# Final residual of a two-layer trunk step: state rows stored to the outputs early, expert rows added there by accumulating transfers

## The reference

```
def trunk_layer(x, cond, p, mixer, rope, ctx):
    sh1, sc1, g1, sh2, sc2, g2 = adaln(cond, p['w_ada'], p['b_ada'])
    h = rms_norm(x, p['g_norm1']) * (1 + sc1) + sh1
    y, state = mixer(h, p, rope, ctx)
    x = x + g1 * y
    h = rms_norm(x, p['g_norm2']) * (1 + sc2) + sh2
    x = x + g2 * hier_moe(h, p)
    return x, state
```

## Time and profile before

| | us |
|---|---|
| median of three runs | 1000.05 |
| the runs | 1000.92, 995.45, 1000.05 |
| the profiled execution | 995.68 |
| its span | 993.9 |

### The profile page before, as it was taken

One profiled execution on the slowest core, in us unless ns is written; L12 is line 12 of the kernel. 1 busy time (PEld: TensorE's weight loads), 2 busy tenths in 40 slices (PEclk: granted clock), 3 DMA queues, 4 the chain that ended last, 5 costly groups with the idle time before them and its releaser, 6 DMA issues.

```text
span 993.9 us, 14410 instructions
## 1 busy us (share of the span) xinstructions
PE 894.8 (90%) x5457; PEld 499.1 (50%) x5457; DVE 407.2 (41%) x1184; ACT 239.6 (24%) x604; POOL 120.1 (12%) x131
## 2 busy tenths in 40 slices
PE   4999889999999999887899998998989999997880
PEld 2345436547555565444356564555655555544440
DVE  2102476346622442211363666564764225321214
ACT  3111144111111111111344455333211111111111
POOL 1000000100222222211100000001001222222120
PEclk9999999999999999999999999999999999998995
DMA  9989799739899999998760029606699999999965
GB/s 374 399 333 404 289 421 416 257 137 363 350 417 417 410 417 418 418 418 315 278 233 6 1 94 377 260 1 189 217 420 400 417 419 408 417 416 419 413 276 197
DMA packets 61685, 318.85 MB, mean 321 GB/s; under 512 B 12598, under 2 KB 13878, under 8 KB 31528
## 3 DMA queue, kind: packets, MB, share of 16 engines
q1 hardware_dynamic: 46144, 285.84, 71.4%
q0 software_dynamic: 13328, 25.02, 7.4%
q10 hardware_dynamic: 2144, 7.06, 1.8%
HBM read 312.72 MB, written 26.49 MB: 341 GB/s over the span
## 4 chain that ended last, share of the span: by engine, by line
PE 65%; DMA 20%; DVE 9%; ACT 2%; issue 2%; SPq 1%; DVEq 0%; POOLq 0%; ACTq 0%
PE psum L916 16%; DMA ring<-in_l_w 15%; PE psum L929 9%; PE psum L1135 7%; PE psum L1247 3%; PE psum L852 3%; PE psum L865 3%; PE psum L896 2%; PE psum L1256 2%; PE psum L696 2%; PE psum L1339 1%; DMA ring<-in_ada_first 1%; PE psum L1361 1%; PE psum L922 1%; PE psum L1288 1%
## 5 line engine op out<-in xcount | busy, mean ns | idle before, releaser
L916 PE MATMUL psum<-ring,scratch 128*64 128x256 f32 x1744 | 210.2, 393 | 25.8 <-DMA ring<-in_l_w 25.7
L916 PEld LDWEIGHTS psum<-ring,scratch 128*64 128x64 f32 x1744 | 135.6, 141 | 85.0 <-issue 37.6
L2254 DVE TENSOR_TENSOR scratch<-scratch,psum 64x256 f32<-64x256 f32 x64 | 27.2, 425 | 291.7 <-ACT scratch L1531 285.9
L929 PE MATMUL psum<-ring,scratch 128*64 128x512 f32 x464 | 112.8, 607 | 1.9 <-ACT scratch L1579 1.0
L2721 POOL DMA_INDIRECT expert_rows<-scratch,slot_rows x64 | 63.5, 991 | 343.1 <-ACT scratch L1545 343.1
L1531 ACT ACTIVATE scratch<-psum 64x256 f32<-64x256 f32 x64 | 24.0, 375 | 260.2 <-PE psum L916 257.0
L1135 PE MATMUL psum<-ring,scratch 128*128 128x512 f32 x192 | 73.5, 540 | 1.5 <-DVE scratch L1862 1.5
L1545 ACT COPY scratch<-psum 128x512 f32<-128x512 f32 x64 | 37.5, 586 | 133.6 <-PE psum L929 133.6
L1135 PEld LDWEIGHTS psum<-ring,scratch 128*128 128x128 f32 x192 | 36.0, 190 | 36.6 <-issue 35.5
L929 PEld LDWEIGHTS psum<-ring,scratch 128*64 128x64 f32 x464 | 29.6, 137 | 42.1 <-issue 37.9
L2236 DVE COPY scratch<-psum 128x512 f32<-128x512 f32 x64 | 41.5, 687 | 7.9 <-PE psum L878 6.8
(11 more groups left out here) (383 smaller groups left out, 1215.0 us busy)
## 6 DMA issues: line engine op xcount, KB each, us to landing
ring<-in_l_w SPq DMA_DIRECT2D x108, 1024.0 KB
ring<-in_l_w_rows SPq DMA_DIRECT2D x56, 1024.0 KB
ring<-in_l_w_ada SPq DMA_DIRECT2D x40, 1024.0 KB, 5.4
ring<-in_ada_first SPq DMA_DIRECT2D x8, 1024.0 KB
ring<-in_l_w_o SPq DMA_DIRECT2D x8, 1024.0 KB
ring<-in_l_w_in SPq DMA_DIRECT2D x4, 1024.0 KB
gate_rows<-gate_rows_hbm POOLq DMA_DIRECT2D x8, 512.0 KB, 7.9
scale_shift<-gate_rows_hbm POOLq DMA_DIRECT2D x8, 512.0 KB, 10.7
```

Source lines behind the costliest of these rows:

```text
L916: last = nc.tensor.matmul(ps[64 * n:64 * n + 64, 2 + par, 0:DE], mine[:, k, :], part(w, k * DE, DE), start=k == 0, stop=k == KD - 1)
L929: last = nc.tensor.matmul(ps[64 * n:64 * n + 64, 5 + par, :], hhT[:, par, k, :], part(w2, k * D + n * 512, 512), start=k == 0, stop=k == 1)
```

## The change

In layer 1, `put_state` stores the tiles to the outputs themselves. The state isn't loaded back. VectorE's addition to x goes; its product with g2 signals x_updated, and GpSimd, which waits for that and for the state's six stores (x_out at 96), adds the tile to the output in HBM with an accumulating DMA. Tile 2 is loaded, scaled, combined and added in two halves of 512 columns; the second half's loads count on x_back. GpSimd waits for the four accumulating DMAs at the end, in ScalarE's place.

```diff
--- before.py
+++ after.py
@@ -376,6 +376,10 @@
 
         def cond_of(t):
             return 0 if t == 0 else 1
+
+        def out_rows(t):
+
+            return (O[1][:, (t - 1) * P:t * P, :] if t else O[0]).rearrange("a s d -> (a s) d")
 
 
         MIX0 = [(t, i) for t in range(NT) for i in range(4)]
@@ -618,7 +622,7 @@
                 sp.wait_ge(S[f"ov_out{l}"], 16)
                 for buf in range(2):
                     sp.wait_ge(S[f"y_out{buf}"], 16 * (l + 1) * PAIRS)
-                for t in range(NT):
+                for t in range(2 if l else NT):
                     for k in range(2):
                         sp.dma_start(pair(t, k), Y[(k * NT + t) * P:(k * NT + t + 1) * P, :]).then_inc(S[f"pair_rows{t}"], 16)
 
@@ -676,8 +680,12 @@
                 if k >= 3 and k < 7:
                     load_wo_unit(1, k - 3)
             load_experts(1)
-            load_state(1)
             load_pairs(1)
+            for hf in range(2):
+                part = slice(hf * 512, (hf + 1) * 512)
+                for k in range(2):
+                    sp.dma_start(pair(2, k)[:, part], Y[(k * NT + 2) * P:(k * NT + 3) * P, part])\
+                        .then_inc(S["x_back" if hf else "pair_rows2"], 16)
 
 
         @block.tensor
@@ -1454,7 +1462,7 @@
 
             def put_state(l, t):
 
-                act.dma_start(X[l][t * P:(t + 1) * P, :], x[:, t, :]).then_inc(S["x_out"], 16)
+                act.dma_start(out_rows(t) if l else X[l][t * P:(t + 1) * P, :], x[:, t, :]).then_inc(S["x_out"], 16)
 
             def evac_h(stage, dst, t):
                 act.wait_ge(S["hT_in_psum"], 3 * stage + t + 1)
@@ -1594,6 +1602,15 @@
 
                 act.wait_ge(S[f"pair_rows{t}"], 32 * (l + 1))
                 nc.scalar.activation(pair(t, 0), pair(t, 0), ACT.Identity, scale=gates[:, t, 0:1]).then_inc(S["pair_scaled"], 1)
+
+            def scale_half(hf):
+
+                if hf:
+                    act.wait_ge(S["x_back"], 48 + 32)
+                else:
+                    act.wait_ge(S["pair_rows2"], 64)
+                part = pair(2, 0)[:, hf * 512:(hf + 1) * 512]
+                nc.scalar.activation(part, part, ACT.Identity, scale=gates[:, 2, 0:1]).then_inc(S["pair_scaled"], 1)
 
             def router(l):
 
@@ -1797,13 +1814,10 @@
             router(1)
             experts(1)
 
-            for t in range(NT):
+            for t in range(2):
                 scale_pair(1, t)
-            for t in range(NT):
-                act.wait_ge(S["x_updated"], 10 + t)
-                dst = O[1][:, (t - 1) * P:t * P, :] if t else O[0]
-                act.dma_start(dst.rearrange("a s d -> (a s) d"), x[:, t, :]).then_inc(S["out_done"], 16)
-            act.wait_ge(S["out_done"], NT * 16)
+            for hf in range(2):
+                scale_half(hf)
             act.wait_ge(S["k_out"], 16)
             act.wait_ge(S["l1_out"], 16)
             act.wait_ge(S["v_out"], 32)
@@ -2360,10 +2374,26 @@
                 link(V.scalar_tensor_tensor(out=p0, in0=p1, scalar=gates[:, t, 1:2], in1=p0,
                                             op0=ALU.mult, op1=ALU.add))
                 dve.wait_ge(S["g2_in"], 32 * (l + 1))
+                if l:
+                    V.tensor_tensor(p0, p0, G[:, cond_of(t), :], ALU.mult).then_inc(S["x_updated"], 1)
+                    return
                 link(V.tensor_tensor(p0, p0, G[:, cond_of(t), :], ALU.mult))
-                dve.wait_ge(S["x_back"], 48 * (l + 1))
+                dve.wait_ge(S["x_back"], 48)
                 V.tensor_tensor(x[:, t, :], x[:, t, :], p0, ALU.add).then_inc(S["x_updated"], 1)
-                dve.wait_ge(S["x_updated"], 6 * l + 4 + t)
+                dve.wait_ge(S["x_updated"], 4 + t)
+
+            def combine_half(hf):
+
+                part = slice(hf * 512, (hf + 1) * 512)
+                p0, p1 = pair(2, 0)[:, part], pair(2, 1)[:, part]
+                if hf:
+                    dve.wait_ge(S["x_back"], 48 + 32)
+                else:
+                    dve.wait_ge(S["pair_rows2"], 64)
+                dve.wait_ge(S["pair_scaled"], 6 + hf)
+                link(V.scalar_tensor_tensor(out=p0, in0=p1, scalar=gates[:, 2, 1:2], in1=p0,
+                                            op0=ALU.mult, op1=ALU.add))
+                V.tensor_tensor(p0, p0, G[:, 1, part], ALU.mult).then_inc(S["x_updated"], 1)
 
 
             V.memset(scT[:, :, :], 0.0)
@@ -2683,8 +2713,10 @@
             norm(3, 2)
             router(1)
             experts(1)
-            for t in range(NT):
+            for t in range(2):
                 combine(1, t)
+            for hf in range(2):
+                combine_half(hf)
 
 
         @block.gpsimd
@@ -2789,6 +2821,15 @@
                         pool.wait_ge(S["up_done"], l * NE + AGAIN[0] + 1)
                         for c in range(2):
                             spread_row(l, 2, 1, c, G[:, c, :], S["g2_in"])
+            pool.wait_ge(S["x_out"], 96)
+            for t in range(2):
+                pool.wait_ge(S["x_updated"], 10 + t)
+                pool.dma_start(out_rows(t), pair(t, 0), accum_op=ALU.add).then_inc(S["out_done"], 16)
+            for hf in range(2):
+                part = slice(hf * 512, (hf + 1) * 512)
+                pool.wait_ge(S["x_updated"], 12 + hf)
+                pool.dma_start(out_rows(2)[:, part], pair(2, 0)[:, part], accum_op=ALU.add).then_inc(S["out_done"], 16)
+            pool.wait_ge(S["out_done"], 4 * 16)
 
 
 def x_after(n):
```

## The result

The changed kernel took 1004.16 us (median of nine runs, 999.2 to 1009.2) against 998.48 us for the kernel before (nine runs, 995.45 to 1001.0). The ratio is 1.0075 with a 95% interval of 1.005 to 1.0101, so 5 to 10 us were lost (the two medians alone would say 5.7). The forecast was 998.7 us and a gain of 1.3.

The account below looks back on a forecast made before the run. TensorE and the weights' queue bound the body, VectorE's chain the tail. VectorE's 2.4 us less 0.3 and 0.3, plus 0.3 for half size, less 0.8 for the addition gave 1.3: 1000.05 becomes 998.7 us, range 993.5 to 1004.

Parts of the forecast that it names:

- part 2: Tail stores move from ScalarE's queue to GpSimd's and accumulate: a gain of 2.1 us with an addition that costs nothing.
- VectorE's end: In the tail, VectorE ends 2.4 us earlier than its 990.79, with two instructions per tile and tile 2 in halves.
- VectorE to issue: In the tail, GpSimd starts a DMA 0.30 us after VectorE's instruction ends, against 0.04 us before.
- issue to landing: The last 256 KB half lands 2.3 us after its issue with nothing added, against 2.6 before; the addition costs 0.8.
- landing to end: At the kernel's end, GpSimd answers the last completion in place of ScalarE, some 0.3 us slower.
- The addition: Accumulating stores in the tail cost between nothing and the destination's bytes moved again, 2.56 us per tile; 0.8 us taken.
- Rival C: In the tail, GpSimd's path, the addition and tile 2's late loads eat all the gain: about 0, 1000.0; chance 0.12.
- Rival A: The four accumulating transfers limit the tail in place of VectorE: 1003.2 us at 4.1 us per 512 KB; chance 0.25.
- The reload: Three state loads of 512 KB behind the last weights go: gain taken as 0, with 0.9 us as its end.
- Rival B: The state's reload held up the weights before the last expert: with 0.9 us back, -2.2 us, 997.9; chance 0.15.
- Exclusion of GpSimd by VectorE: By the skill's rule, the first half's descriptors wait for VectorE's end, the second's come 0.57 us late: gain 0.7 us.
- Over 23.3 us: Mark of being wrong: tail from last scatter to span's end, 23.3 us before, under 21 or over 23.3.

Follow-up runs that it names:

- e2: The changed kernel with ScalarE waiting for the four accumulating transfers in GpSimd's place: tail 27.7 us, ratio to the kernel before 1.0051.
- e3: The changed kernel with plain stores from GpSimd in place of accumulating ones, state left out of the outputs: tail 28.0 us, ratio to the kernel before 1.0051.
- e4: The changed kernel with plain stores issued and awaited by ScalarE, state left out of the outputs: tail 19.7 us, ratio to the kernel before 0.9972.
- e6: The changed kernel with plain stores issued by GpSimd and awaited by ScalarE, state left out of the outputs: tail 26.2 us, one run.
- d1: The changed kernel with two early DRAINs on GpSimd, which still waits for the accumulating transfers: tail 24.8 us, ratio to the kernel before 1.0016.
- d2: The changed kernel with two early DRAINs on GpSimd and ScalarE waiting for the accumulating transfers: tail 23.4 us, ratio to the kernel before 1.0008.
- e1: The kernel before with the wait for the final stores moved from ScalarE to the end of GpSimd's program: tail 30.2 us, ratio 1.0064.
- h0: The kernel before with tile 2 loaded, scaled, combined and stored by ScalarE in halves, reload kept: tail 23.1 us, ratio 1.0004.
- h1: The kernel before with tile 2 in halves and tile 0 alone added by one accumulating GpSimd transfer: tail 22.2 us, ratio 1.0011.

## Why the prediction was wrong

The step that failed is one clause of part 2, "GpSimd then answers the completion in place of ScalarE, some 0.3 us slower by the same lag". I priced the answer and not what GpSimd does behind it: 7.5 us of DRAIN. The answer itself was quick, the DRAIN began 0.2 us after the landing. The evidence was in the trace of before, an 8.4 us record on GpSimd's queue at 970.4, hidden there by the tail. Among "what is queued behind GpSimd's new waits" I listed only its own stores. The terms of the tail, measured against forecast:

| term | forecast | measured |
|---|---|---|
| VectorE's end | -2.4 | -3.1 |
| VectorE to issue | +0.3 | +0.3 |
| issue to landing | +0.5 (256 KB -0.3, addition +0.8) | +2.7 |
| landing to end | +0.3 | +7.5, all of it the DRAIN |
| sum | -1.3 | +7.4 |

**VectorE.** The mechanism was right and the halves measured 0.75 and 0.69 us for 0.74 and 0.69. Of the further 0.7 us, 0.5 come from tile 1: its pair was there sooner after SyncE's first issue (7.8 us against 8.25), so the gap ahead of it was 0.5 us, forecast as 0.9. That is this one profile: in those of e2, e3, e4, e6, d1 and d2, which have the same VectorE program, VectorE ended 16.9 to 18.2 us after the scatter, on both sides of the forecast's 17.8.

**The addition** was mis-sized: 3.1 us at the last half (e3 against the changed kernel) for 0.8. Per byte it takes twice the engines' time, the upper of the two values that I placed, and the later transfers queue behind one another. Even the first tile's, with no addition ahead of it, landed after 5.4 us against 3.1 plain in e3, where doubling its bytes' 1.28 us explains 1.3 of the 2.3 us; the rest isn't explained. The Trainium skill, "Collectives: The Full Stack", in the section on the bandwidth ceiling, has the adding ReduceScatter at half the rate of the copying AllGather, since an addition reads two sources; the trace agrees with the factor, 193 to 203 GB/s against 410, and doesn't show the reason. But the last landing came 22.7 us after the scatter, where I had placed it at 22.0 with that rate (992.6 less 970.64) and a later VectorE; so the addition ate all that VectorE gave. Rival C described this part, and d2, with the DRAIN off the path, ends at its price: zero. Rival A's place was right in that the transfers and not VectorE set the last landing, but not its price; it would have needed 3.1 us per 512 KB, and 512 KB at 200 GB/s take 2.6. That the measured 1004.16 us lies next to A's 1003.2 is chance: the DRAIN, which A doesn't have, made the loss.

**The reload.** Rival B's sign, a shrinking last wait of TensorE for weights, doesn't show. With the reload this wait was 0.9 us before and in e1, and 2.2 in h0; without it 0.7 to 0.9 us in e2, e3, e4, d1 and d2, and 2.2 in e6 and in the changed kernel (ahead of 955.17). It takes one of two sizes in either case, and the totals, with intervals about 4 us wide, couldn't tell 0.9 us.

**Exclusion of GpSimd by VectorE.** The first half's issue, beside VectorE's instructions, took 0.83 us, and the second's, behind VectorE's end, 0.84: no stretch shows. The Trainium skill, "SBUF — State Buffer", section "SBUF: two separate sides", keeps GpSimd from writing descriptors during a two-port instruction of VectorE, while instructions with two SBUF inputs shut out only a GpSimd instruction that reads SBUF. The prediction ran the two together to get its gain of 0.7 us; nothing shows that VectorE's instructions here, which have two SBUF inputs, are two-port ones.

My chances gave 0.13 to a loss of over 0.5%, for another mechanism. "Over 23.3 us" for the tail was the mark of being wrong, and at 30.6 it was met.

## What to carry to other kernels

The engine that waits for the last transfer should be one whose program then ends at once: here ScalarE closed in 8 ns and GpSimd in 7.5 us. Before work is moved to GpSimd's end, ask the profile for the closing instructions of each engine, which neither the busy times nor the chain of waits show; a DRAIN put early, where GpSimd idles and its transfers have landed, takes the cost off the end (d1, d2). An addition made by a DMA ran at half the rate of a store, so its place is an early tile and not the last one: in h1 that took 1.0 us off the tail, too little to show in the total.

## What was not expected of the hardware

GpSimd's DRAIN cost 0.08 to 0.09 us for each of its DMAs since the last DRAIN (0.14 us for one, 3.3 for forty), and at 113 of them without a DRAIN GpSimd stopped once for 2.8 us more than usual by itself. In the large kernel, with 98 indirect and 28 direct ones, it came to 7.2 us, less than 126 times 0.08; whether and where a limit was met there isn't shown. A DRAIN also outlasted GpSimd's own transfers in flight: begun behind the last issue in d2, with four DMAs to pay for, it ended 0.2 us after their landing, and with 127 and 130 (h1, e2) 3.6 and 3.8 us after it. An accumulating transfer also takes GpSimd longer to issue, 0.84 to 0.97 us against 0.55 to 0.59 for the same plain one.
